# Linear attention's projections as three products of split operands, a residual spilled tile by tile, and cached rows copied in another stage

## What is computed

```
h = rmsnorm(y) @ w_in_odd            # q, k: 512 columns each; v, r: 1024 each; gd: 16
logg = log_sigmoid(gd @ gate_up + gate_b) / 16
step over chunks of 64 tokens, for each of 4 heads (q, k of 128, v of 256 columns):
    b = cumsum(gc);  A = (qc * exp(b_t - b_s)) . kc        # causal
    o = A @ vc + (qc * exp(b)) @ S
    S = exp(b_last) * S + (kc * exp(b_last - b)).T @ vc
out = rmsnorm(o) * silu(r)
y = y + out @ w_out_odd;  y = y + swiglu(rmsnorm(y), gate, up, down)
```

## Time and profile before

| | us |
|---|---|
| median of three executions | 3733.22 |
| the profiled execution | 3734.27 |
| its span, first to last instruction | 3732.6 |
| around the span | 1.7 |
| PE busy | 3461.6 |
| stage of GLA, by the trace | 2279 to 2824 |

### The profile page before, as it was taken

How to read it: one execution, slowest core, us unless ns; L and a number is a source line. 1 busy time by engine, 2 the same in 40 slices (tenths; PEclk the granted TensorE clock), 3 DMA queues, 4 the chain that set the end, 5 groups by cost and what they waited for, 6 DMA issues and landing times. The chain is left out here.

```text
span 3732.6 us, 62216 instructions
## 1 busy us (share of the span) xinstructions
PE 3461.6 (93%) x25987; PEld 2872.3 (77%) x25987; DVE 1466.3 (39%) x2698; ACT 831.2 (22%) x1576; POOL 560.1 (15%) x384
## 2 busy tenths in 40 slices
PE   8888887898878869999999998999997999999999
PEld 5666656554446559999999996666657999999999
DVE  5465665422466663323232233422324332322322
ACT  2233222011356523111111111322212211111110
POOL 0000000204000004222222212000002322222221
PEclk9899998899699979999999999999998999999999
DMA  2000100403200041111111102111123111111111
GB/s 102 21 30 10 34 13 20 145 22 86 69 1 1 10 160 47 45 45 39 44 51 40 40 28 113 35 47 53 42 95 117 48 52 37 48 35 45 51 40 65
DMA packets 74665, 189.20 MB, mean 51 GB/s; under 512 B 27148, under 2 KB 41420, under 8 KB 71388
## 3 DMA queue, kind: packets, MB, share of 16 engines
q1 hardware_dynamic: 61148, 156.92, 12.2%
q0 software_dynamic: 8960, 28.32, 2.3%
q10 hardware_dynamic: 4352, 1.05, 0.1%
HBM read 161.34 MB, written 29.04 MB: 51 GB/s over the span
## 5 line engine op out<-in xcount | busy, mean ns | idle before, releaser
L178 PE MATMUL ps<-ff_x,ff_wh 128*128 128x384 f32 (+1 forms) x3960 | 774.9, 328 | 0.0
L178 PEld LDWEIGHTS ps<-ff_x,ff_wh 128*128 128x128 f32 x3960 | 668.8, 188 | 0.8
L178 PE MATMUL ps<-ff_x,ff_wl 128*128 128x384 f32 (+1 forms) x2112 | 465.5, 328 | 0.0
L178 PEld LDWEIGHTS ps<-ff_x,ff_wl 128*128 128x128 f32 x2112 | 360.8, 188 | 0.0
L525 DVE TENSOR_TENSOR resid<-resid,ps 128x384 f32 (+1 forms) x240 | 113.3, 528 | 386.8 <-PE ps L178 386.8
L2556 PE MATMUL ps<-act,gl_w 128*128 128x384 f32 (+1 forms) x768 | 244.3, 473 | 0.0
L178 PE MATMUL ps<-ff_hh,ff_dh 128*128 128x384 f32 (+1 forms) x1056 | 233.4, 329 | 7.2 <-DVE ff_hl L517 4.6
L178 PE MATMUL ps<-ff_hh,ff_dl 128*128 128x384 f32 (+1 forms) x1056 | 232.7, 328 | 0.0
L178 PE MATMUL ps<-ff_hl,ff_dh 128*128 128x384 f32 (+1 forms) x1056 | 232.7, 328 | 0.0
L2556 PEld LDWEIGHTS ps<-act,gl_w 128*128 128x128 f32 x768 | 144.1, 192 | 90.2 <-issue 10.5
L512 DVE TENSOR_TENSOR ff_prod<-ff_silu,ps 128x384 f32<-128x384 f32 x132 | 62.3, 528 | 349.6 <-PE ps L178 349.6
(11 more groups left out here) (607 smaller groups left out, 5425.2 us busy)
## 6 DMA issues: line engine op xcount, KB each, us to landing
ff_w<-in_wg SPq DMA_DIRECT2D x44, 512.0 KB, 3.5
ff_w<-in_wu SPq DMA_DIRECT2D x44, 512.0 KB, 3.5
ff_wd<-in_wd POOLq DMA_DIRECT2D x48, 256.0 KB, 3.0
ff_wd<-in_wd POOLq DMA_DIRECT2D x32, 320.0 KB, 3.3
rw_w<-in_w_rwkv SPq DMA_DIRECT2D x14, 512.0 KB, 3.6
ns_past<-in_cache_slc SPq DMA_DIRECT2D x48, 128.0 KB, 2.1
np_w<-in_w_nsa SPq DMA_DIRECT2D x8, 652.0 KB, 10.6
resid<-in_x SPq DMA_DIRECT2D x1, 4352.0 KB, 14.8
```

What stands on the lines that cost most here:

```text
L178: mm = pe.matmul(g.ps[:, bank + c, 0:n], w[:, k, :], x[:, o:o + n], start=(first and i == 0), stop=(last and i == 2))
```

## The change

Six parts:

1. K, Q, R, G and V are computed with three fp32r matmuls for each f32 one. 25 units of weights (G, and K, Q, A, B, R, S for the heads; A and B are halves of V's) are loaded into two staging buffers, copied to `high` by ACT and subtracted into `low` by POOL, in three slots. The first two are loaded by SP, the others by POOL behind its subtraction of the unit two places earlier. The steps at which ACT and POOL convert a unit are listed in `next_units`.
2. The normalization writes a draft, ACT rounds it into `act_high` and DVE subtracts it into `resid_low`, which lies in the memory of the residual. ACT rounds the tiles in pieces between its other steps. G waits for each k-tile.
3. The residual is stored tile by tile at the end of layer 0's feed-forward, and read back in eight DMAs late in phase 3, after the states' stores and before the last store of the gated output.
4. `v`, `at` and `kt` get one buffer each, `e`, `qs` and the draft share memory, gating is done in place, and V7 and V8 are placed later in the middle phases.
5. The window rows are copied in the first eight iterations of layer 0's feed-forward loop.
6. Only the constants that GLA uses are loaded for it, and POOL clears the semaphores of the first projection.

```diff
@@ output_and_feed_forward, SP
+            for a, z in ((1, 1 + NB), (1 + NB, FT)):
+                with sp.Fori(a, z) as i:
...
+                    if layer == 0 and a == 1:
+                        sp.dma_start(win_to[ds(i - 1, 1)], win_from[ds(i - 1, 1), 8:512, :]).then_inc(g.window_copied, 16)
+            for t in range(KT):
+                sp.wait_ge(s.down_out, D0 + (len(PARTS) - 1) * KT + t + 3)
+                sp.dma_start(resid_to[:, t, :], g.resid[:, t, :]).then_inc(g.resid_stored, 16)
@@ the same, DVE, ahead of the residual additions
+            if layer == 1:
+                dve.wait_ge(g.resid_back, 16 * KT)
@@ gla_heads, order of the middle phases
-    middle = ("... S5 V2 V3 S6 V4 V5 S7 V6 V7 S8 V8 R0 S9 "
+    middle = ("... S5 V2 V3 S6 V4 V5 S7 V6 S8 V7 S9 V8 R0 "
@@ which units are converted at which step
+    def next_units(h, x):
+        first_of = 6 * h + 5
+        listed = {(-1, "G2"): [3], (-1, "K2"): [4], (-1, "Q2"): [5], (-1, "V8"): [6, 7]}
+        if h >= 0 and h < 3:
+            listed |= {(h, "K2"): [first_of + 3], (h, "Q2"): [first_of + 4], (h, "V8"): [first_of + 5, first_of + 6],
+                       (h, "R2"): [first_of + 7], (h, "R5"): [first_of + 8] if h < 2 else []}
@@ SP
-            sp.dma_start(g.spilled, g.resid[:, :, :]).then_inc(g.tokens_moved, 16)
...
+                    sp.dma_start(d.gl_s[h], b.st8[:, :, :]).then_inc(st8_stored, 16)
...
+                if h == 3:
+                    full(sp, 3, "R5")
+                    for k in range(KT):
+                        sp.dma_start(g.resid[:, k, :], g.spilled[:, k, :]).then_inc(g.resid_back, 16)
@@ POOL
+            def low(u):
+                pool.wait_ge(s.high_done, u + 1)
+                if u >= GLA_SLOTS:
+                    used(pool, u - GLA_SLOTS)
+                pool.tensor_tensor(b.low[:, u % GLA_SLOTS, :, :], b.stage[u % 2][:, :, :], b.high[:, u % GLA_SLOTS, :, :].bitcast(F32), ALU.subtract)\
+                    .then_inc(s.low_done, 1)
+                if u + 2 < len(units):
+                    pool.wait_ge(s.low_done, u + 1)
+                    pool.dma_start(*weights(u + 2)).then_inc(here[u % 2], 16)
@@ PE
-                    mm = pe.matmul(out[:, 0:n], w[:, k, :], g.act[:, k, o:o + n], start=(k == 0), stop=(k == KT - 1))
+                    if opening:
+                        norm.normed.next(pe)
+                    for i, (w, act) in enumerate(((wh, xh), (wl, xh), (wh, xl))):
+                        mm = pe.matmul(out[:, 0:n], w[:, k, :], act[:, k, o:o + n], start=(k == 0 and i == 0), stop=(k == KT - 1 and i == 2))
...
+                    for j, (act, w) in enumerate(((xh, wh), (xh, wl), (xl, wh))):
+                        mm = pe.matmul(out[:, 0:256].rearrange("p (a n) -> p a n", a=2), act[:, k, tok], w[:, :, k, :],
+                                       start=(k == 0 and j == 0), stop=(k == KT - 1 and j == 2))
@@ ACT
+            def high(u):
+                act.wait_ge(*((first_here[u], 16) if u < 2 else (here[u % 2], 16 * (u // 2))))
+                if u >= GLA_SLOTS:
+                    used(act, u - GLA_SLOTS)
+                    act.wait_ge(s.low_done, u - GLA_SLOTS + 1)
+                act.activation(b.high[:, u % GLA_SLOTS, :, :], b.stage[u % 2][:, :, :], ACT.Copy).then_inc(s.high_done, 1)
...
+            high(0)
+            rounded(0, early)
+            high(1)
+            rounded(0, late)
+            high(2)
+            rounded(1, early)
+            beside = {"G0": (1, late), "K0": (2, early), "Q0": (2, late)}
@@ DVE
+                for k in range(KT + 1):
+                    if k < KT:
+                        signal.drafted.mark(dve.scalar_tensor_tensor(b.draft[:, k, 0:n], g.resid[:, k, o:o + n], gain[:, k:k + 1], rs[:, c, 0:n],
+                                                                     ALU.mult, ALU.mult))
+                    if k >= 1:
+                        signal.rounded.next(dve)
+                        norm.normed.mark(dve.tensor_tensor(g.resid_low[:, k - 1, o:o + n], b.draft[:, k - 1, 0:n],
+                                                           g.act_high[:, k - 1, o:o + n].bitcast(F32), ALU.subtract))
```

More of the change, by code:

```diff
@@ L2488, in gla_heads, with weights, used @@
     rows = lambda t: P if t < 8 else NS
+    units = gla_units()
+    unit = {}
+    for h in phases:
+        n = h + 1
+        if h < 0:
+            unit[h, "G"] = units.index("G")
+        if n < 4:
+            for kind, name in (("K", "K"), ("Q", "Q"), ("V", "A")):
+                unit[h, kind] = units.index(f"{name}{n}")
+        if 0 <= h < 4:
+            unit[h, "R"] = units.index(f"R{h + 1}") if h < 3 else len(units) - 2
+    def weights(u):
+        name, to = units[u], b.stage[u % 2]
+        n = int(name[1]) if len(name) > 1 else 4
+        if name == "G":
+            return to[:, :, 64:80], d.w_gla_gd
+        if name[0] in "QK":
+            return to[:, :, :], d.w_gla_qk[n + 4 * (name[0] == "K")]
+        if name[0] in "AB":
+            o = P * (name[0] == "B")
+            return to[:, :, :], d.w_gla_v[n, :, :, o:o + P]
+        return to[:, :, :], d.w_gla_r[2 * (n - 1) + (name[0] == "S")]
+    def used(eng, u):
+        name = units[u]
+        n = int(name[1]) if len(name) > 1 else 4
+        if name == "G":
+            full(eng, -1, "G2")
+        elif name[0] in "KQ":
+            full(eng, n - 1, name[0] + "2")
+        elif name[0] in "AB":
+            full(eng, n - 1, "V8")
+        else:
+            full(eng, n - 1, "R2" if name[0] == "R" else "R5")
+    def next_units(h, x):
[4 more added lines that the diff above has]
+                       (h, "R2"): [first_of + 7], (h, "R5"): [first_of + 8] if h < 2 else []}
+        return [u for u in listed.get((h, x), []) if u < len(units)]
     with nc.Block() as block:
@@ new lines, in _ @@
+            pool.memset(b.stage[0][:, :, :], 0.0).then_inc(s.cleared, 1)
+            for u in range(GLA_SLOTS):
+                low(u)
+            pool.wait_ge(g.const_here, 32)
+            for h in phases:
+                n = h + 1
+                for x in sequence(h):
+                    if x == "F8":
+                        pool.wait_ge(keys.sem, n + 1)
+                        if n:
+                            pool.wait_ge(o_ready.sem, 9 * n)
+                        qe8_ready.mark(pool.tensor_tensor(b.qe8[:, :, :], b.qe[n % 2][:, NP:TOK].unsqueeze(1).to_broadcast([P, NB, NS]), g.bcol, ALU.mult))
+                        consumed(pool, h, "F8")
+                        if n:
+                            pool.wait_ge(outer.sem, 10 * n)
+                        kt8_ready.mark(pool.tensor_tensor(b.kt8, b.kt[0:NS, 8, :].unsqueeze(1).to_broadcast([NS, NB, P]),
+                                                          g.brow[0:NS, :].unsqueeze(2).to_broadcast([NS, NB, P]), ALU.mult))
+                    for u in next_units(h, x):
+                        low(u)
@@ L2629, in _ @@
                     if kind == "G":
[L2630 to L2633 removed]
+                        dense(h, x, unit[h, "G"], t, out, True)
                     if kind == "L":
```

249 lines of the change are left out of this document (118 added, 131 removed).

## The result

The changed kernel takes 3695.02 us (median of 4 runs), the kernel before 3734.01 beside it: a ratio of 0.9892, with a 95% interval of 0.9879 to 0.9906. That is 39.0 us less; the forecast was 44 less, 3689, with a range of 3670 to 3716. The profiled execution took 3693.8 us, its span is 3692.1, 40.5 less than the span before.

The account below looks back on a forecast made before the run. PE was taken to bound the kernel, busy for 93% of the span. The terms 66 - 12.6 - 2.7 - 1.5 - 8 + 2.7 = 43.9 us, off a median of 3733.2, gave about 3689, range 3670 to 3716.

Parts of the forecast that it names:

- Matmuls, 66 us: GLA's K, Q, R, G and V tiles: fp32r triples replacing f32 matmuls save 66 us of PE time.
- (a): Rival, V tiles in GLA: weight loads set the pace, V saves nothing, 22 us less gained, 3711; chance 0.15.
- (d): Rival, V tiles in GLA: V's fp32r matmuls are not single passes, 267 us more, 3956; chance 0.04.
- (e): Rival, GLA's new matmuls: weight loads run in series with matmuls, by the skill's figures; chance 0.01.
- Opening, -12.6: GLA's start: 7 us idle before L0, 2 more for the clock, 3.6 before V0; 12.6 lost, from 6 to 18.
- L0 stands behind the taking of G1: GLA's opening: PE idles before L0 until ACT takes G1, after the doubled normalization; 7 us lost.
- V4 ... is covered still: GLA's opening: exponentials end 21.5 us after G2's taking, V4 needs V0's bank only at 23.9, so no wait.
- Spill, -1.5: End of layer 0's feed-forward: residual stores share DMA engines with POOL's low weights; 0 to 3 us, taken as 1.5 lost.
- End, -8: GLA's end: residual loads delay the gated output's last store, bounded by 5 and 11 us, taken as 8 lost.
- Window rows, +2.7: After the recurrent unit: PE's 2.66 us wait for np_w goes, 2.7 gained; copies hidden in the feed-forward loop.
- (b): Rival, GLA's opening and end: both losses are hidden after all, 3676; chance 0.14.
- (c): Rival, GLA's weight conversions: the chain through ACT and POOL reaches PE, 81 us added, 3770; chance 0.05.

Follow-up runs that it names:

- run 3: Changed kernel with only the 16 filled columns of unit G converted by ACT and POOL, zeros written into the others beforehand: 3685.47 us (0.9863).
- run 8: Changed kernel with K2 ahead of L1 and L2 in GLA's first phase and DVE's logs at Q2's place: 3686.39 us (0.9874).
- run 4: Changed kernel with unit B of the next head converted at Q1's place, not K2's, in the middle phases: 3686.57 us (0.9871).
- run 6: Changed kernel with the first six residual stores held back until the sixth tile at the end of layer 0's feed-forward: 3682.42 us (0.9866).
- run 2: Changed kernel with the eight residual loads issued right behind the last head's gl_p store, once R5 is filled: 3680.38 us (0.985).
- run 7: Changed kernel with the window rows copied in the recurrent unit's SP queue again, not in the feed-forward's loop: 3695.92 us (0.9895).
- run 9: Changed kernel with K2 ahead of L1 and L2, and ACT's first-phase exponentials and unit 5's conversion moved to V3's place: 3678.67 us (0.9851).
- run 5: Changed kernel with unit B of the next head converted at Q0's place, not K2's, in the middle phases: 3681.83 us (0.9864).
- run 1: The changed kernel once more, with no edit: 3690.33 us (0.9882).

## Why the prediction was right, point by point

- **Matmuls, 66 us: right.** 68 by the tiles. V costs 2.93 a tile, where 2.94 was reckoned; its pace of 0.118 us lies between the bounds, near pure streaming (0.107), and (a), (d) and (e) fall with it. By an estimate from the figures of the Trainium skill ("TensorE: Matmul & The Clock Gate", Back-to-back issue gap and LDWEIGHTS) a load of 107 ns in series with a matmul of 107 would have shown 0.214. The page itself has the two pipelined, and the trace, at 0.118, agrees with that and contradicts the series.
- **Opening, -12.6: the size nearly, the mechanism partly wrong.** Nine tiles of K, Q and G and nine of V should have saved 6 x 0.99 + 3 x 0.73 + 9 x 0.61 = 13.6, and 4.0 came: 9.6 lost. The wait of V0 for unit 4 was 4.08, predicted 3.6. The 7 us "L0 stands behind the taking of G1" was wrong: L0 needs only its own G0 taken and a free bank, which G0 frees too. It ran at 2311.36, while ACT took G1 at 2316.78, as late as predicted (2315) and waited for by nobody. In its place stood 2.2 us of waits inside G0 for DVE, behind the second of the two held subtractions shown at run 3, and 6.8 us more at half clock, 3.4 of time, for 2 predicted. "V4 ... is covered still" was right by 0.8 us only: ACT had taken V0 at 2349.1, and V4 began at 2349.9. The exponentials ended 23.5 us after G2's taking, not 21.5, since the scan before them took 4.40 us for 2.42 beside POOL's subtraction of unit 4. Run 8 showed what lies behind this margin.
- **Middle phases: a term was missing.** S9's waits, 2.7 predicted, were 2.0 (5.7 us in four waits, of which 3.7 was there before). But POOL's conversions, costed at nothing beside other work, hold DVE's copies and its instructions with two inputs in SBUF; through copy and gating that reached PE in phases 1 and 2 for 4.4 us of wait and 3.4 of clock. Run 4 gave 7 of it back.
- **Spill, -1.5: mis-sized.** 3.5 (run 6); the bound of 3 was too low because a half-clock piece behind the waits was not reckoned.
- **End, -8: right**, 8.05 in run 2, by the mechanism named.
- **Window rows, +2.7: mis-sized.** 6.7 between the two kernels, 4.9 by run 7; the 1.8 between these stay open. The wait for `np_w` was priced alone; the later start of the whole stage and the starved first tile were not.
- **Rivals.** (b) fell with the opening and the end as they are. Its 3676 does not follow from its own terms either: without the 12.6 and the 8 the forecast of 3689 becomes 3668, below the stated range. (c) came true only in its gentlest form: PE never waited for `gl_low` in a middle phase, but POOL reached it by way of DVE.

The sum: 68 - 9.6 - 10 (middle phases: 49 saved by their tiles, 39.0 seen) - 7.7 (end) = 40.7 in GLA; 6.7 for the window rows, -3.5 for the spill, -2.1 and -1.0 in stretches that the change doesn't touch: 40.8, for the 40.5 of the span. Errors of both signs met. Against the forecast the matmuls gave 2 more, the opening 3.0 and the window rows 4.0; the middle phases gave 7.3 less and the spill 2.0, and 3.1 were lost where nothing was changed. That the total came within 4 us of 43.9 is in part luck; the largest term and the end were right by their mechanisms.

## What to carry to other kernels

Work that moves to an idle POOL isn't free for DVE: put its conversions where DVE reads PSUM or waits, and look for DVE instructions much longer than their twins. A transfer needed later goes to where its place comes free, not to where the queue happens to reach it, and never in front of the store that ends the stage. Before pricing "A waits for B", read which count the wait compares; and before curing a wait, see what would wait next: run 8 removed 4 us and lost 2, while the pair of run 9 gained 6.

## What the runs showed of the hardware

- **POOL and DVE hold each other, in some instructions.** A DVE copy of 16 columns took 2.15 us for 0.17 beside a POOL subtraction, a DVE subtraction of 384 columns 2.39 and 2.67 for 0.55, a shift of 64 columns 2.42 for 0.22, each ending 0.03 to 0.41 us after POOL's; a scan took 4.40 for 2.42. POOL's took 3.05 for 2.35 when it began under a scan of DVE. A DVE instruction with an operand in PSUM was not held (run 5), and neither was a reciprocal in SBUF (2.55 us at 2296.6 in the changed kernel, with a POOL subtraction of 2.36 beside it). No wait is recorded for any of this; only the lengths show it. The Trainium skill ("SBUF — State Buffer", Who interferes with whom) says just this: "only the shared port pair causes contention, and it's an exclusive lock", for DVE instructions with two inputs in SBUF and for copies in a mode that uses both ports. The rows here agree, and it bore on this change before it was made.
- **A short wait of PE costs more than itself.** In the changed kernel's GLA a piece of 3.4 us at a granted clock of 0.5 lies behind the waits of 1.83, 4.08, 2.21, 2.22 and 3.30 us, and each costs 1.7; behind one of 2.15 us in the feed-forward there is none. In run 4 a wait of 2.2 us removed gave 3.5 back per phase. Such pieces also come and go between executions of one kernel (run 1), which makes up much of the scatter of its totals.
- **An fp32r matmul of 256 columns, given as two pieces of 128, with a load of 128 columns for each, keeps a pace of 0.118 us.** From 384 to 320 to 256 columns the pace falls by 0.028 each time (0.174, 0.146, 0.118), so down to 256 the load sets no floor.
